# A two-block transformer kernel on one core: three modulation slabs beside each early projection, and half of four output blocks accumulated beside the second attention

## What is computed

```python
# both blocks: six modulation vectors per condition, from a 1024 x 6144 matrix
mod = silu(cond) @ w_ada + b_ada
h   = rms(x, g) * (1 + scale) + shift
# block 1
pl, pc = split_in(h_lat @ w_in), split_in(h_ctx @ w_in)     # q, k, v, o, gates of a gated linear attention; q, k, v of a window attention
m, a   = mlstm(pl, pc), window_attention(pl, pc)            # 8 heads x 2 tiles of 128 queries
x = x + g1 * ((sigmoid(g_m) * (m @ w_bm) + sigmoid(g_a) * (a @ w_ba)) @ w_out)
x = x + g2 * peer(modulate(x))      # per token 8 x 16 rows fetched from a table of 16384
# block 2
attn = na_latent(q, k, v, kc, vc, rpb)                      # again 8 heads x 2 tiles
conv = b * short_conv(c * h, w_conv)
x = x + g1 * (concat([fourier(f) @ w_fourier, attn, conv]) @ w_out)
x = x + g2 * hier_moe(modulate(x))  # 32 experts, 2 per token
out = rms(x, norm_final)
```

## Time and profile before

| | us |
|---|---|
| median of 3 runs | 1656.39 |
| lowest, highest | 1656.16, 1660.06 |
| the profiled execution's own time | 1654.45 |
| its span (first to last instruction) | 1652.6 |
| TensorE busy / weight loads | 1347.8 / 775.1 |
| VectorE, ScalarE, GpSimd busy | 780.2, 452.7, 316.1 |
| moved by DMA | 583.53 MB, 353 GB/s over the span |

### The profile page before, as it was taken

The page is one execution under the profiler, slowest core; times in us unless marked ns, Lnnn a source line. Parts: engine busy times, 40 slices in busy tenths (PEclk is TensorE's granted clock), DMA queues, the critical chain, the costliest instruction groups (busy, mean ns, idle before and its releaser), DMA issues.

```text
span 1652.6 us, 19061 instructions
## 1 busy us (share of the span) xinstructions
PE 1347.8 (82%) x7112; PEld 775.1 (47%) x7112; DVE 780.2 (47%) x1887; ACT 452.7 (27%) x1235; POOL 316.1 (19%) x272
## 2 busy tenths in 40 slices
PE   5999999998878888779798887799996665666666
PEld 3467886697435554335344542386841221221122
DVE  2101774427687776788888786627320010010001
ACT  2111214412354433454544443215110000000001
POOL 0000000003344333454454455202000000000000
PEclk7999999999999998899999999999997897898897
DMA  9557236946999999999999999953589999999997
GB/s 396 225 200 300 102 106 262 407 168 282 422 420 420 422 416 413 423 412 413 416 421 421 403 422 421 372 204 120 217 345 427 428 428 427 427 428 427 428 428 303
DMA packets 61713, 583.53 MB, mean 353 GB/s; under 512 B 6848, under 2 KB 7232, under 8 KB 8256
## 3 DMA queue, kind: packets, MB, share of 16 engines
q1 hardware_dynamic: 23040, 302.99, 44.5%
q0 software_dynamic: 36864, 268.45, 39.2%
q10 hardware_dynamic: 1728, 11.03, 1.7%
HBM read 581.39 MB, written 1.05 MB: 352 GB/s over the span
## 4 chain that ended last, share of the span: by engine, by line
PE 41%; DMA 39%; DVE 11%; ACT 4%; issue 3%; POOL 1%; SPq 0%; ACTq 0%; DVEq 0%; PEldq 0%
PE ps L1101 37%; DMA big<-peer_uv,big 16%; DMA slab<-w_stream 13%; DMA big<-w_stream 6%; DVE big L2221 4%; DMA scratch<-w_stream 4%; PE ps L1347 1%; POOL big L674 1%; PE ps L1355 1%; ACT big L927 1%; ACT big L923 1%; DVE big L2232 1%; DVE stat L2097 1%; DVE big L2169 0%; PE ps L1258 0%
## 5 line engine op out<-in xcount | busy, mean ns | idle before, releaser
L1101 PE MATMUL ps<-big 128*128 128x512 f32 (+2 forms) x2054 | 618.2, 570 | 171.5 <-ACT big L927 116.1
L1101 PEld LDWEIGHTS ps<-big 128*128 128x128 f32 (+1 forms) x2054 | 257.0, 178 | 489.2 <-ACT big L927 207.0
L674 POOL DMA_INDIRECT big<-peer_uv,big x256 | 305.1, 1192 | 746.9 <-DVE big L2205 385.8
L2221 DVE CUSTOM_DVE_ANT_0 big<-big 128x1024 f32<-128x1024 f32 x256 | 310.6, 1225 | 122.8 <-DMA big<-peer_uv,big 117.6
L1101 PE MATMUL ps<-xh,slab 128*128 128x128 f32 (+1 forms) x1152 | 172.3, 309 | 1.1 <-ACT xh L724 1.1
L1101 PEld LDWEIGHTS ps<-xh,slab 128*128 128x128 f32 x1152 | 161.0, 197 | 20.7 <-issue 11.7
L1101 PE MATMUL ps<-slab,big 128*32 128x512 f32 x768 | 114.9, 728 | 64.8 <-DMA slab<-w_stream 63.3
L919 ACT ACTIVATE big<-big 128x1 f32<-128x1 f32 x256 | 51.5, 201 | 331.2 <-DVE big L2221 330.9
L2441 DVE TENSOR_TENSOR big<-big,ps 128x512 f32<-128x512 f32 x8 | 5.5, 687 | 228.9 <-PE ps L1101 228.9
L1101 PEld LDWEIGHTS ps<-slab,big 128*32 128x32 f32 x768 | 24.0, 120 | 144.4 <-DMA slab<-w_stream 87.1
L1101 PE MATMUL ps<-slab,xh 128*128 128x256 f32 (+2 forms) x304 | 89.5, 450 | 2.3 <-DMA slab<-w_stream 2.3
(11 more groups left out here) (345 smaller groups left out, 1236.5 us busy)
## 6 DMA issues: line engine op xcount, KB each, us to landing
slab<-w_stream SPq DMA_DIRECT2D x90, 2048.0 KB, 17.4
big<-w_stream SPq DMA_DIRECT2D x35, 2048.0 KB, 32.4
scratch<-w_stream SPq DMA_DIRECT2D x8, 2048.0 KB, 32.2
slab<-w_stream SPq DMA_DIRECT2D x8, 1024.0 KB, 30.5
scratch<-w_stream SPq DMA_DIRECT2D x8, 1024.0 KB, 31.2
big<-w_stream ACTq DMA_DIRECT2D x2, 2048.0 KB, 14.6
big<-peer_uv,big POOLq DMA_INDIRECT x256, 11.3
big<-w_stream SPq DMA_DIRECT2D x2, 1024.0 KB, 6.0
```

The source lines that it names most:

```text
L674: nc.gpsimd.indirect_dma_start(out=uv[b], out_offset=None, in_=peer_uv, in_offset=bass.IndirectOffsetOnAxis(ap=idxu[:, s:s + 1], axis=0)). ...
L1101: ins = nc.tensor.matmul(*a, **kw)
L2221: V.tensor_tensor_reduce(out=u, in0=u, in1=xtok, scale=1.0, scalar=0.0, op0=ALU.mult, op1=ALU.add, accum_out=dots[:, s:s + 1]).then_inc(do ...
```

## The change

The first part moves ada slabs. Three of them now follow each early projection instead of two (12 early, not 8), so the stream has K, V, GKV and Q as slabs 4, 8, 12 and 16; in `attention(0)` one ada slab stands at each even unit and its turn at the next odd one (8, not 12). The number of slabs in the stream, and all from the modulation's last slab on, stay. The third row of a stage reuses PSUM bank 6, after ScalarE's copy of the first.

The second part moves matmuls of the second block's output projection. Of blocks j = 0 to 3, the products over k = 0, 1, 6 and 7 (16 matmuls of 128 x 256) run one after each unit of `attention(1)`, into banks 6 and 7; after the attention these blocks need k = 2 to 5 only. The router's matmuls, the turned tokens and the rows of gains get other banks, the router's calls stand one block later, and `row(0)` no longer waits for `turn_stored`.

```diff
@@
-S_K, S_V, S_GKV, S_Q = (ADA_FIRST + 3 * i for i in range(4))
-ADA_EARLY = 8
+ADA_STAGE = 3
+S_K, S_V, S_GKV, S_Q = (ADA_FIRST + (1 + ADA_STAGE) * i for i in range(4))
+ADA_EARLY = 4 * ADA_STAGE
 ADA_MIXED = ADA_FIRST + ADA_EARLY
-S_AQ, S_O, S_MG = S_Q + 3, S_Q + 4, S_Q + 5
+S_AQ, S_O, S_MG = (S_Q + 1 + ADA_STAGE + i for i in range(3))
@@
     if n < ADA_MIXED:
-        return S_K + 3 * ((n - ADA_FIRST) // 2) + 1 + (n - ADA_FIRST) % 2
+        return S_K + (1 + ADA_STAGE) * ((n - ADA_FIRST) // ADA_STAGE) + 1 + (n - ADA_FIRST) % ADA_STAGE
@@
-        ada_buf = [at(scratch, i * T, T) for i in range(2)]
+        ada_buf = [at(scratch, i * T, T) for i in range(ADA_STAGE)]
@@
+        def y2(j):
+
+            return bank(6 + j // 2, T, j % 2 * T) if j < 4 else bank(j - 4, T)
+
+        def y2_filled(j):
+            return 2 * KD + (1, 1, 2, 2, 3, 4, 5, 6)[j]
+
@@
-            return n if n < 8 else n - 8 if n < 10 else n - 10
+            return n if n < 8 else (0, 1, 6, 7, 1, 2)[n - 8]
         Y0_BANKS = (0, 1, 2, 4)
+        ROW_BANKS = (3, 0)
@@ ScalarE
             def early_rows(i):
-                for j in range(2):
-                    ada_row(ADA_FIRST + 2 * i + j, ada_buf[j], 6 + j)
+                for j in range(ADA_STAGE):
+                    ada_row(ADA_FIRST + ADA_STAGE * i + j, ada_buf[j], 6 + j % 2)
@@
-                    if blk == 0 and u % 4 != 3:
-                        ada_row(ADA_MIXED + u // 4 * 3 + u % 4, hcT[:, 0:T])
+                    if blk == 0 and u % 2 == 0:
+                        ada_row(ADA_MIXED + u // 2, hcT[:, 0:T])
@@ TensorE
             def early_turns(i):
-                for j in range(2):
-                    ada_turn(ADA_FIRST + 2 * i + j, ada_buf[j], 5 * 512 + 8 * j)
+                for j in range(ADA_STAGE):
+                    ada_turn(ADA_FIRST + ADA_STAGE * i + j, ada_buf[j], 5 * 512 + 8 * j)
 
             def early_rows(i):
-                for j in range(2):
-                    n = ADA_FIRST + 2 * i + j
-                    ada_rows(weights(ada_slab(n)), 0, 6 + j)
+                for j in range(ADA_STAGE):
+                    n = ADA_FIRST + ADA_STAGE * i + j
+                    if j == 2:
+                        pe.wait_ge(adarow_stored, n - 1)
+                    ada_rows(weights(ada_slab(n)), n // ADA_SLABS, 6 + j % 2)
@@
                 for u in range(first, first + UNITS):
                     if blk == 0:
-                        n = ADA_MIXED + u // 4 * 3 + u % 4
-                        if u:
-                            ada_turned(n - 1)
-                        if u % 4 != 3:
+                        n = ADA_MIXED + u // 2
+                        if u % 2:
+                            ada_turn(n, hcT[:, 0:T])
+                        else:
                             ada_rows(weights(ada_slab(n)), 1)
                     turn_probs(u)
@@
                     if u > first:
                         apply(u - 1)
+                    if beside is not None:
+                        beside(u - first)
@@
-            attention(1, last_projection)
+            def out2_early(i):
+                ks, j, k = i // 8 * 6, i % 8 // 2, i % 2
+                if i == 4:
+                    pe.wait_ge(bank_emptied, unit[0])
+                if i == 8:
+                    pe.wait_ge(conv_ready, 1)
+                w = weights(S_OUT2).rearrange("p (k n) -> p k n", k=KD)
+                mm(y2(j), w[:, ks + k, j * P:(j + 1) * P], catT[:, (ks + k) * T:(ks + k + 1) * T],
+                   start=(ks + k, j % 2) == (0, 0), stop=False, skip_group_check=True)
+
+            attention(1, last_projection, out2_early)
@@
             for j in range(KD):
                 w = weights(S_OUT2 + j // 4).rearrange("p (k n) -> p k n", k=KD)
-                chain(bank(7, T) if j == KD - 1 else bank(j // 2, T, j % 2 * T), by_feature(catT, w, j % 4),
-                      y_filled if j % 2 or j == KD - 2 else None)
+                if j < 4:
+                    for k in range(2, 6):
+                        mm(y2(j), w[:, k, j * P:(j + 1) * P], catT[:, k * T:(k + 1) * T], start=False, stop=k == 5,
+                           skip_group_check=True, signal=y_filled if (j % 2, k) == (1, 5) else None)
+                else:
+                    chain(y2(j), by_feature(catT, w, j % 4), y_filled)
                 if j % 4 == 3:
                     slab_done()
-                if j in (3, 5):
-                    router(j - 3)
-                    router(j - 2)
+                for k in ((), (), (), (0, 1), (2, 3), (), (4,), ())[j]:
+                    router(k)
                 if j == 5:
                     turn_tokens(0)
-                if j == KD - 2:
-                    router(4)
-                    router(5)
-            router(6)
-            router(7)
+            for k in (5, 6, 7):
+                router(k)
             turn_tokens(1)
@@
-            pe.wait_ge(turn_stored, 11)
             row(0)
             pe.wait_ge(rexp_in, 1)
             open_sums(0)
+            pe.wait_ge(norm_inv, 8)
+            row(1)
             pe.wait_ge(turn_stored, 14)
-            row(1)
@@ VectorE
-                    if blk == 0 and u and (u - 1) % 4 != 3:
-                        ada(ADA_MIXED + (u - 1) // 4 * 3 + (u - 1) % 4)
+                    if blk == 0 and u % 2:
+                        ada(ADA_MIXED + u // 2)
```

More of the change, by code:

```diff
@@ L1037, in row_out @@
                 act.wait_ge(grow_filled, half + 1)
-                nc.scalar.activation(g2_row[:, half * 512:(half + 1) * 512], bank((0, 3)[half]),
+                nc.scalar.activation(g2_row[:, half * 512:(half + 1) * 512], bank(ROW_BANKS[half]),
                                      ACT.Copy).then_inc(grow_stored, 1)
@@ L1321, in _, with attention @@
                 turn(2 + n, [k[:, c * P:(c + 1) * P] for c in (2, 3, 0, 1)])
-            def attention(blk, beside_first=None):
+            def attention(blk, beside_first=None, beside=None):
                 first = blk * UNITS
@@ L1365, in apply @@
                                                for c in range(4)], head_filled)
-                def ada_turned(n):
-                    if n >= mixed[0]:
-                        ada_turn(n, hcT[:, 0:T])
-                        mixed[0] = n + 1
-                mixed = [ADA_MIXED]
                 scores(first)
@@ L1637, in router @@
                     for t in range(NT):
-                        mm(bank(6, 1, t), square_at(7, i)[:, t * P:(t + 1) * P], ones[:, 0:1], start=(i, t) == (0, 0),
+                        mm(bank(0, 1, t), square_at(7, i)[:, t * P:(t + 1) * P], ones[:, 0:1], start=(i, t) == (0, 0),
                            stop=i == KD - 1, skip_group_check=True,
@@ L1665, in row @@
                 pe.wait_ge(diag2_ready, half + 1)
-                mm(bank((0, 3)[half]), ones, g2_diag[half], start=True, stop=True, signal=grow_filled)
+                mm(bank(ROW_BANKS[half]), ones, g2_diag[half], start=True, stop=True, signal=grow_filled)
             def open_sums(t):
@@ L1870, in _, with early_ada @@
             bg = rowv("b_gates").rearrange("p (d g h) -> p d g h", d=2, g=2)
-            for n in range(ADA_FIRST, ADA_FIRST + 4):
-                ada(n, 5, 8 * (n % 2))
+            def early_ada(first, end):
+                for n in range(ADA_FIRST + first, ADA_FIRST + end):
+                    ada(n, 5, 8 * ((n - ADA_FIRST) % ADA_STAGE))
+            early_ada(0, 2 * ADA_STAGE)
             dve.wait_ge(late_loaded, 32)
@@ L1884, in _ @@
             step(V.tensor_scalar(lf, fg, 0.0, None, ALU.min))
-            for n in range(ADA_FIRST + 4, ADA_FIRST + 6):
-                ada(n, 5, 8 * (n % 2))
+            early_ada(2 * ADA_STAGE, 3 * ADA_STAGE)
             dve.wait_ge(soft_ready, 1)
             V.tensor_tensor(lf, lf, soft, ALU.subtract).then_inc(lf_ready, 1)
-            for n in range(ADA_FIRST + 6, ADA_MIXED):
-                ada(n, 5, 8 * (n % 2))
+            early_ada(3 * ADA_STAGE, ADA_EARLY)
             dve.wait_ge(cums_filled, 1)
@@ L2326, in _ @@
                     square7(j - 1)
-                dve.wait_ge(y_filled, 2 * KD + 1 + j // 2 + (j == KD - 1))
+                dve.wait_ge(y_filled, y2_filled(j))
                 x = xT[:, j * T:(j + 1) * T]
-                y = bank(7, T) if j == KD - 1 else bank(j // 2, T, (j % 2) * T)
-                V.scalar_tensor_tensor(out=x, in0=y, scalar=modc(1, 2, j), in1=x,
+                V.scalar_tensor_tensor(out=x, in0=y2(j), scalar=modc(1, 2, j), in1=x,
                                        op0=ALU.mult, op1=ALU.add).then_inc(x_updated, 1)
@@ L2341, in _ @@
             dve.wait_ge(norm_sum, 8)
-            step(V.tensor_scalar(rms2, bank(6, NT),
+            step(V.tensor_scalar(rms2, bank(0, NT),
                                  1.0 / D, EPS, ALU.mult, ALU.add))
```

## The result

The changed kernel takes 1671.35 us (median of 5 runs, 1668.46 to 1677.91), 15.0 us or 0.92% more than the kernel before; the ratio is 1.0092 with a 95% interval of 1.0069 to 1.0114. The forecast was 1665.4 us. Its sign was right, its size was 6 us short, and the range ended at 1671.5. The profiled execution took 1668.46 us with a span of 1666.7, 14.1 more than the span of before.

The account below looks back on a forecast made before the run. Two long stages were taken as DMA-bound and merely shifted, leaving TensorE's path through projections and attentions to decide. Terms +10.4 + 10.3 + 3.7 - 12.8 - 1.7 - 0.9 = +9.0 us on 1656.39 gave 1665.4, range 1658.5 to 1671.5.

Parts of the forecast that it names:

- four slabs' rows and turns beside the projections: Early projections: each added ada slab costs TensorE 2.59 us for rows, turn and wait for VectorE; four make +10.4.
- three late projection slabs: Early projections: V, GKV and Q wait 3.2, 3.0 and 4.1 us for their loads, +10.3, bounds 9.0 to 12.3.
- clock in the early stages: Early projections: idle waits lower TensorE's granted clock; two falls of 1.85 us counted, +3.7, bounds 0 and 6.9.
- first attention: First attention: four units take 13.23 us instead of 16.42, with fewer slabs and no 0.89 wait; -12.8 in all.
- `w_branch_m` late: First attention's end: this load has 13.7 us left; 0 taken as fewer slabs compete for DMA, 1.2 otherwise.
- fetch of expert rows and the start of block 2: The DMA-bound fetch of expert rows lasts as long as before and only shifts: 0.
- second attention longer: Second attention: added matmuls make a pair of units last about 5.0 us instead of 4.31, with 1.7 us absorbed in all.
- 16 matmuls out of the projection, `row(0)`: Behind the second attention: sixteen matmuls leave the output projection, 7.0 us less; `row(0)` not waiting for ScalarE gives -0.9.
- a clock that holds: Rival, early projections: the waits come but the clock doesn't fall, +5.3, 1661.7 us; chance 0.13.
- The main mechanism: Early projections: K, V, GKV and Q share `slab0`, so each load waits for the previous projection and lands late; +10.3.
- the two added waits beside the second attention: Second attention: waits for ScalarE emptying the last gate projection and for GpSimd's convolution cost nothing.
- the third row's wait for ScalarE: Early projections: the third row's wait for ScalarE's copy is covered by the second slab's 1.80 us, so costs nothing.

Follow-up runs that it names:

- `p1_move_alone`: The changed kernel with its second part undone, so only the ada slabs are moved: 1678.42 us, ratio 1.0143 to the kernel before.
- `branch_early`: The changed kernel with the load of `w_branch_m` issued at the ninth unit of the first attention, not the twelfth: 1666.01 us.
- `side_three`: The changed kernel with the slabs of projections V, GKV and Q loaded into two buffers of their own: 1655.38 us.
- `side_spread`: The kernel with two extra buffers for V, GKV and Q, its three turns a stage set apart instead of in a row: 1647.86 us.
- `late_v`: The kernel before, with only the load of projection V's slab held until projection K is used up: 1664.25 us.
- `side_one`: The changed kernel with a buffer of its own for projection V's slab alone; GKV and Q still wait: 1670.15 us.

## Why the prediction was right in sign and short in size

Term by term, from the two profiled executions:

| term | forecast, us | measured, us |
|---|---|---|
| four slabs' rows and turns beside the projections | +10.4 | +10.9 |
| three late projection slabs | +10.3 | +11.1 |
| clock in the early stages | +3.7 | +8.9 |
| first attention | -12.8 | -13.7 |
| `w_branch_m` late | 0 | +1.9 |
| fetch of expert rows and the start of block 2 | 0 | +0.9 |
| second attention longer | +5.3 | +3.0 |
| 16 matmuls out of the projection, `row(0)` | -7.9 | -8.1 |
| the rest, to the end | 0 | -0.7 |
| sum | +9.0 | +14.2 |

The clock's row is what is left of the +30.9 at the first attention after 10.9 and 11.1.

- **The step that failed: "I count two falls of 1.85, +3.7, with bounds of 0 and 3 x 2.3 = 6.9."** It measured 8.9, over its own upper bound. That is 5.2 us too little, as much as the sum was short; the other misses cancel. By groups the 8.9 are 1.6, 1.7 and 3.0 behind the three waits, 1.7 behind Q's three turns (159.38), and the 0.9 by which the fall that the kernel before has at 149.25 grew. So there were three falls behind the waits and not two, and two places that the term left out. Not all of it is the same each time: in `p1_move_alone` and `branch_early`, whose early stages are the same, the same sum is 5.7 (three falls of 1.4 to 1.7, and the 0.9), which is within the bounds and still 2 us over the forecast. The other 3.2 us, the longer fall behind Q's wait and the one behind its turns, came in one of these three executions, that of the changed kernel. What the term costs on average no trace here shows; the other four executions of the changed kernel, which have none, took 2 to 9 us longer than the one traced. That rows of three turns can cost the clock at all is shown by `side_three` against `side_spread`, 3 of 3 against none. The matmul at full speed after 1.91 us of idling, which spoke for a clock that holds, said little: 14 of 15 waits of 3 to 5 us did lower it.
- **The main mechanism was right.** Three waits for loads of `slab0`, 3.5, 3.9 and 3.8 us for 3.2, 3.0 and 4.1, landings of 8.0, 8.4 and 8.3 for 7.8, 7.6 and 8.7. `late_v` gives 4.85 for 5.0 by the same working. The fit in the Trainium skill, "DMA: Bandwidth & Descriptors", section "Anatomy of one DMA — SWDGE (gpsimd) path", gives an estimate of 6.8 us for 2 MB, by which each wait would have been 2.2 us; every landing here was longer.
- **"I take 0, since fewer slabs compete for DMA; 1.2 if they don't help."** Wrong: the load of `w_branch_m` took 15.2 us, not less than the 14.9 of before, and had 13.3.
- **The first attention** gave its 0.89 us of waiting as said, and a little more, 12.65 for four units instead of 13.23.
- **The second attention** was over-priced: a pair at 5.0, measured 4.78. The idle 0.18 us a pair in the earlier trace rows isn't all the slack: before the change, 1.01 us lay between the start of the second application's last matmuls and the next turn, and 0.67 between the same starts of the first application; the difference is 0.34. That is most of the 0.41 us that a pair absorbed (0.88 of matmuls added, 0.47 longer). The end of a group is modelled, so slack is read from start to start.
- **Costed at nothing and right:** the two added waits beside the second attention, the third row's wait for ScalarE, and the DMA-bound stages, within 1 us in these two executions. Over all kernels the stretch from the fetch to the second attention moves by 5 us, so part of this agreement is luck.

Left open: which part of a row of turns lowers the clock, its waits of 0.35 us or its small matmuls. No kernel here has a row of turns without the waits. A single turn behind a wait of 0.89 us, in the first attention of the kernel before, was followed by no fall (granted clock 1.00 from 276 to 296 us). Open too is why the same early stages show 0 or 3.4 us at the lower level from one execution to another, and 23.9 or 17.0 after the change, and why all six rows of three turns in `side_three` and `side_one` were followed by a fall but only two of the twelve others.

## What to carry to other kernels

In a ring of buffers, the number of slabs between two big ones decides which buffer the next comes into. With four buffers and three small slabs after each big one, every big load waits for the big one before it, and the small ones must cover issue plus landing: here 5.4 us against 9. Two more buffers for these three loads gave back 16 us. And a wait on TensorE costs what the clock does behind it too, here 6.3 us beside 11.1 of waits (4.9 and 4.8 beside 11.2 and 10.7 in two other executions of the same stages), and the clock took 2.6 us more elsewhere. Count a fall behind every such wait, and every place where TensorE's work thins out, short turns in a row among them, and not the waits alone.

## What the hardware showed that was not expected

- Seven useless matmuls in each of three waits made the kernel 6.5 us faster, as the groups behind them ran in 14.00, 7.60 and 7.17 us instead of 15.62, 9.27 and 10.19.
- Taking one wait away moved the falls of the clock instead of removing one: 30.9 us at the lower level in the profiled execution of `side_one`, 23.9 and 17.0 in those with one wait more.
- One wait of 3.32 us of 15 such passed without a fall.
- The stretch from the first fetch of expert rows to the second attention, the same work in every kernel, took 731.6 to 736.7 us from one profiled execution to another, as much as some of the differences between kernels here.
